# Latent attention's heads in pairs, two heads' outputs at a time, gates before roots, fillers moved

## What is computed

```
s = einsum('bhqd,bhkd->bhqk', qblk, k) * scale;  p = softmax(s);  o = einsum('bhqk,bhkv->bhqv', p, v)

a = where(incl, einsum('bhnid,bhnjd->bhnij', q_dec, k_inv), 0);  o_intra = einsum('bhnij,bhnjv->bhniv', a, v)
def step(s, xs):                                   # per chunk
    o = einsum('bhcd,bhdv->bhcv', qd_c, s)
    s = s * ge_c[..., None] + einsum('bhcd,bhcv->bhdv', ke_c, v_c)

gla = rms_norm(gla, o_norm) * silu(gg)             # even layer
o   = rms_norm(o, o_norm) * silu(g)                # odd layer
rms_norm(x, w) = x * rsqrt(mean(x * x) + EPS) * w
```

## Time and profile before

| | |
|---|---|
| runs | 2077.41, 2098.91, 2096.75 us, median 2096.75 |
| profiled execution | 2104.82 us, span 2103.0 us |
| busy shares | PE 94%, PEld 83%, DVE 55%, ACT 49%, POOL 7% |
| mean granted clock of TensorE | 0.977 of 2.4 GHz |
| DMA | 254.55 MB, mean 121 GB/s |

### The profile page before, as it was taken

The page is one execution under the profiler, slowest core; times in us unless marked ns, Lnnn a source line. Parts: engine busy times, 40 slices in busy tenths (PEclk is TensorE's granted clock), DMA queues, the critical chain, the costliest instruction groups (busy, mean ns, idle before and its releaser), DMA issues.

```text
span 2103.0 us, 40763 instructions
## 1 busy us (share of the span) xinstructions
PE 1983.4 (94%) x16442; PEld 1737.9 (83%) x16442; DVE 1164.9 (55%) x1809; ACT 1030.9 (49%) x1624; POOL 156.6 (7%) x151
## 2 busy tenths in 40 slices
PE   6999999899999999999889999999989998999997
PEld 5884588787788788878778889999879998788997
DVE  4421578654643343355345667667757656667654
ACT  5333367634432233244644456555747655356653
POOL 0000100001000000100044310010020001011000
PEclk9999999889999999999999999999999999899999
DMA  8340268541233333232200056665436664325653
GB/s 270 96 125 30 70 207 249 156 121 50 80 93 97 90 91 99 83 99 82 71 4 4 24 144 187 183 186 145 132 100 188 186 179 138 101 66 145 186 174 110
DMA packets 441801, 254.55 MB, mean 121 GB/s; under 512 B 10817, under 2 KB 440513, under 8 KB 441537
## 3 DMA queue, kind: packets, MB, share of 16 engines
q1 hardware_dynamic: 441664, 252.59, 41.0%
HBM read 251.51 MB, written 1.05 MB: 120 GB/s over the span
## 4 chain that ended last, share of the span: by engine, by line
PE 84%; DVE 9%; ACT 4%; issue 2%; DMA 1%; POOL 0%; DVEq 0%; ACTq 0%; SPq 0%; POOLq 0%
PE bank L380 21%; PE bank L382 20%; PE bank L381 20%; PE bank L372 4%; PE bank L601 2%; PE bank L602 2%; DVE weights_lo L330 2%; ACT weights_hi L323 1%; PE bank L939 1%; PE bank L1170 1%; PE bank L1980 1%; PE bank L609 1%; DVE h L2604 1%; DMA ring<-ada_w 1%; PE bank L2005 1%
## 5 line engine op out<-in xcount | busy, mean ns | idle before, releaser
L330 DVE TENSOR_TENSOR weights_lo<-ring,weights_hi 128x1024 fp32r<-128x1024 f32 x472 | 578.2, 1229 | 353.5 <-ACT weights_hi L323 349.4
L323 ACT ACTIVATE weights_hi<-ring 128x1024 fp32r<-128x1024 f32 x472 | 495.7, 1054 | 383.8 <-PE bank L382 359.4
L380 PE MATMUL bank<-x_hi,weights_hi 128*128 128x256 f32 (+1 forms) x2024 | 639.0, 316 | 31.9 <-DVE x_lo L2560 11.0
L381 PE MATMUL bank<-x_lo,weights_hi 128*128 128x256 f32 (+1 forms) x2024 | 629.0, 311 | 0.0
L382 PE MATMUL bank<-x_hi,weights_lo 128*128 128x256 f32 (+1 forms) x2024 | 628.6, 311 | 0.0
L380 PEld LDWEIGHTS bank<-x_hi,weights_hi 128*128 128x128 f32 x2024 | 381.2, 188 | 67.5 <-issue 27.8
L382 PEld LDWEIGHTS bank<-x_hi,weights_lo 128*128 128x128 f32 x2024 | 381.7, 189 | 23.6
L381 PEld LDWEIGHTS bank<-x_lo,weights_hi 128*128 128x128 f32 x2024 | 381.9, 189 | 23.0 <-issue 1.4
L380 PE MATMUL bank<-hidden_hi,weights_hi 128*128 128x256 f32 (+1 forms) x864 | 270.4, 313 | 5.7 <-DVE hidden_lo L2881 3.2
L382 PE MATMUL bank<-hidden_hi,weights_lo 128*128 128x256 f32 (+1 forms) x864 | 269.9, 312 | 0.0
L381 PE MATMUL bank<-hidden_lo,weights_hi 128*128 128x256 f32 (+1 forms) x864 | 268.5, 311 | 0.0
(11 more groups left out here) (358 smaller groups left out, 2338.3 us busy)
## 6 DMA issues: line engine op xcount, KB each, us to landing
ring<-mlp_w SPq DMA_DIRECT2D x128, 512.0 KB, 3.9
ring<-ada_w SPq DMA_DIRECT2D x96, 512.0 KB, 4.6
ring<-w_ffn_in SPq DMA_DIRECT2D x88, 512.0 KB, 4.0
ring<-w_ffn_out SPq DMA_DIRECT2D x32, 512.0 KB, 3.6
ring<-gdn_w_in SPq DMA_DIRECT2D x24, 512.0 KB, 3.9
ring<-even_w_in SPq DMA_DIRECT2D x18, 512.0 KB, 4.1
ring<-w_out SPq DMA_DIRECT2D x16, 512.0 KB, 3.7
ring<-w_in_a SPq DMA_DIRECT2D x14, 512.0 KB, 3.8
```

What stands on the lines that cost most here:

```text
L323: nc.scalar.activation(w_hi[:, g % AHEAD, :], ring[:, g % RAW, :], ACT.Copy).then_inc(hi_done[g % AHEAD].sem, 1)
L330: nc.vector.tensor_tensor(w_lo[:, g % AHEAD, :], ring[:, g % RAW, :], w_hi[:, g % AHEAD, :].bitcast(F32), ALU.subtract).then_inc(lo_done[g ...
L380: pe.matmul(dst, lhs[0](k), rhs[0](k), start=start and k == 0, stop=False)
L381: pe.matmul(dst, lhs[0](k), rhs[1](k), start=False, stop=False)
```

## The change

- `Attention` for the even layer goes through heads in pairs: for each query block an even and an odd head after one another. The value products of both are issued after the second one, alternating between them, into the two partition halves of one bank, with one signal and one copy of 128 partitions. There are four buffers for transposed probabilities.
- GLA's outputs are made for two heads at once: the score products of both, fillers, the wait for the states, then the state products of both heads alternately, in banks 2 and 3. Heads 2 and 3 wait until both banks are copied.
- In both mixers DVE multiplies outputs by norm weight and gate first, then by the root. In the odd layer logarithms and exponentials alternate.
- Fillers are added, moved ahead of waits or made fewer.

```diff
@@ -615,6 +615,8 @@
                         late()
+                    if t == 2:
+                        keep_busy(pe, 3, 10)
                     if t < self.n // 2:
@@ -911,11 +913,11 @@
-                self.units, self.scale, self.p, self.pt = units, scale, room[0:2], room[2:4]
+                self.units, self.scale, self.p, self.pt = units, scale, room[0:2], room[2:6]
                 n = len(units)
-                self.b = {s.sem: s.take(n) for s in (att_scores, att_max, att_exp, att_probs, att_turned, att_probsT,
-                                                    att_mixed, att_out)}
-                self.masked = room[4:6]
+                self.b = {s.sem: s.take(n) for s in (att_scores, att_max, att_exp, att_probs, att_turned, att_probsT)}
+                self.b |= {s.sem: s.take(n // 2) for s in (att_mixed, att_out)}
+                self.masked = room[6:8]
                 self.before = Linear.last
@@ -939,7 +941,7 @@
                     if j == 0:
-                        keep_busy(pe, 1, 3)
+                        keep_busy(pe, 1, 11)
                     if j >= 0:
@@ -949,13 +951,17 @@
                         side.pe(pe, i)
-                    if j >= 0:
-                        u = self.units[j]
+                    if j >= 0 and j % 2 == 1:
+                        pair = j // 2
                         self.wait(pe, att_probsT, j)
-                        self.wait(pe, att_out, j - 2)
-                        r = u["rows"]
-                        product(pe, bank[j % 2][r, 0:P], lambda b: u["v"][b], lambda b: self.pt[j % 2][:, b * P:(b + 1) * P],
-                                len(u["v"])).then_inc(att_mixed.sem, 1)
+                        self.wait(pe, att_out, pair - 2)
+                        nb = len(self.units[j]["v"])
+                        for b in range(nb):
+                            for x in (j - 1, j):
+                                u = self.units[x]
+                                ins = pe.matmul(bank[pair % 2][u["rows"], 0:P], u["v"][b], self.pt[x % 4][:, b * P:(b + 1) * P],
+                                                start=b == 0, stop=b == nb - 1)
+                        ins.then_inc(att_mixed.sem, 1)
@@ -980,11 +986,10 @@
                         ins.then_inc(att_max.sem, 1)
-                    if i >= 2:
-                        j = i - 2
-                        self.wait(dve, att_mixed, j)
-                        nc.vector.tensor_copy(self.units[j]["out"], bank[j % 2][self.units[j]["rows"], 0:P])\
-                            .then_inc(att_out.sem, 1)
+                    if i >= 2 and i % 2 == 1:
+                        pair = (i - 2) // 2
+                        self.wait(dve, att_mixed, pair)
+                        nc.vector.tensor_copy(self.units[i - 2]["out"], bank[pair % 2][:, 0:P]).then_inc(att_out.sem, 1)
                     if side is not None:
@@ -1005,8 +1010,8 @@
                         self.wait(act, att_turned, j)
-                        self.wait(act, att_mixed, j - 2)
-                        nc.scalar.activation(self.pt[j % 2][:, 0:nk], bank[6 + j % 2][:, 0:nk], ACT.Copy)\
+                        self.wait(act, att_mixed, (j - 4) // 2)
+                        nc.scalar.activation(self.pt[j % 4][:, 0:nk], bank[6 + j % 2][:, 0:nk], ACT.Copy)\
                             .then_inc(att_probsT.sem, 1)
@@ -1024,21 +1029,23 @@
-        room = [a[:, 2 * i, :] for i in range(4)]
+        room = [a[:, i, :] for i in range(6)]
         mla_units = []
         for q0, k0, kn in ((0, 0, T), (LAT, LAT, CTX)):
-            for hd in range(MH):
+            for first in range(0, MH, 2):
                 for q in range(q0, q0 + LAT, P):
-                    r = slice((hd % 2) * MV, (hd % 2 + 1) * MV)
-                    mla_units.append(dict(q=qT[0:MQK, hd, q:q + P], k=kT[0:MQK, hd, k0:k0 + kn],
-                                          v=[vt[:, b, hd * MV:(hd + 1) * MV] for b in range(k0 // P, (k0 + kn) // P)],
-                                          rows=r, out=mix[r, hd // 2, q:q + P]))
+                    for par in range(2):
+                        hd = first + par
+                        mla_units.append(dict(q=qT[0:MQK, hd, q:q + P], k=kT[0:MQK, hd, k0:k0 + kn],
+                                              v=[vt[:, b, hd * MV:(hd + 1) * MV] for b in range(k0 // P, (k0 + kn) // P)],
+                                              rows=slice(par * MV, (par + 1) * MV), out=mix[:, first // 2, q:q + P]))
         mla = Attention(mla_units, MQK ** -0.5, room)
         def pe_mla(pe):
             def ready(pe, i):
-                hd = i * P // LAT
-                if i % (LAT // P) == 0 and hd < MH:
+                hd = 2 * (i // 4) + i % 2
+                if i % 4 < 2 and hd < MH:
                     pe.wait_ge(rope_done.sem, 2 + hd // 2)
...
@@ -1151,25 +1158,27 @@
                 pair(i)
-            keep_busy(pe, 4, 13)
-            for hd in range(GH):
-                f, hh = hd // 2, hd % 2
-                if hd == 0:
+            for f in range(GH // 2):
+                if f > 0:
+                    pe.wait_ge(G["outs"], 2 * f)
+                for hh in range(2):
+                    hd = 2 * f + hh
+                    for tb in range(TB):
+                        pe.matmul(bank[2 + hh][:, tb * P:(tb + 1) * P], gv[:, tb, hd * P:(hd + 1) * P], ascore[:, hd, tb, :],
+                                  start=tb == 0, stop=False, skip_group_check=True)
+                if f == 0:
+                    keep_busy(pe, 4, 9)
                     pe.wait_ge(G["states"], 2 * GFB)
-                    pe.wait_ge(G["masked"], 4 * GFB)
-                if hd >= 2:
-                    pe.wait_ge(G["outs"], hd - 1)
-                b = bank[2 + hd % 2]
-                for tb in range(TB):
-                    t = slice(tb * P, (tb + 1) * P)
-                    pe.matmul(b[:, t], gv[:, tb, hd * P:(hd + 1) * P], ascore[:, hd, tb, :], start=tb == 0, stop=False,
-                              skip_group_check=True)
                 for z in range(2):
                     for n in range(1, NCH):
                         c = ORDER[z][n]
-                        ins = pe.matmul(b[:, chunk(c)], states[z][half(hh), f, n, :], qdec[half(hh), GFB * z + f, chunk(c)],
-                                        start=False, stop=z == 1 and n == NCH - 1, skip_group_check=True)
-                ins.then_inc(G["sums"], 1)
+                        for hh in range(2):
+                            ins = pe.matmul(bank[2 + hh][:, chunk(c)], states[z][half(hh), f, n, :],
+                                            qdec[half(hh), GFB * z + f, chunk(c)], start=False, stop=z == 1 and n == NCH - 1,
+                                            skip_group_check=True)
+                            if z == 1 and n == NCH - 1:
+                                ins.then_inc(G["sums"], 1)
             for hd in range(GH):
@@ -1275,11 +1284,13 @@
             for hd in range(GH):
+                dve.wait_ge(G["outs"], hd + 1)
+                nc.vector.scalar_tensor_tensor(out=mix[:, 4 + hd, :], in0=gout[:, hd, :], scalar=vector("gla_o_norm"),
+                                               in1=gg[:, hd, :], op0=ALU.mult, op1=ALU.mult).then_inc(G["gated"], 1)
+            for hd in range(GH):
+                dve.wait_ge(G["gated"], hd + 1)
                 dve.wait_ge(G["roots"], GH + hd + 1)
-                link(dve, nc.vector.scalar_tensor_tensor(out=mix[:, 4 + hd, :], in0=gout[:, hd, :],
-                                                         scalar=vector("gla_o_norm"), in1=groot[:, hd, :],
-                                                         op0=ALU.mult, op1=ALU.mult))
-                nc.vector.tensor_tensor(mix[:, 4 + hd, :], mix[:, 4 + hd, :], gg[:, hd, :], ALU.mult).then_inc(G["merged"], 1)
+                nc.vector.tensor_tensor(mix[:, 4 + hd, :], mix[:, 4 + hd, :], groot[:, hd, :], ALU.mult).then_inc(G["merged"], 1)
@@ -1524,7 +1535,7 @@
         def pe_rest0(pe):
-            keep_busy(pe, 4, 15)
+            keep_busy(pe, 4, 12)
             pe.wait_ge(G["roots"], GH)
...
@@ -1708,10 +1719,10 @@
                 lin, i = (odd_lin, n) if n < NB_CONV else (sg_lin, n - NB_CONV)
+                if n == 2:
+                    keep_busy(pe, 3, 8)
                 odd_tiles.wait(pe, n)
                 width = odd_width(n)
-                if n == 2:
-                    keep_busy(pe, 3, 7)
                 lin.free(pe, i)
@@ -1938,9 +1949,10 @@
                 pe.wait_ge(gdn_tables.sem, 16)
+                pe.wait_ge(OS["logs"], 2 * QKB)
+                keep_busy(pe, 2, 7)
                 pe.wait_ge(OS["cumsd"], 2)
                 pe.wait_ge(OS["ktok"], QKB)
-                keep_busy(pe, 7, 4)
             for z, u in units(p):
...
@@ -2440,22 +2452,25 @@
                 nc.scalar.activation(as_heads(obuf(osq, i)), two_heads(i), ACT.Square).then_inc(OT["squares"], 1)
-            for i in range(4):
```

(37 more changed lines are left out.)

## The result

| | kernel before | changed kernel |
|---|---|---|
| median (fastest to slowest) | 2098.05 us (2077.41 to 2102.24), 6 runs | 2064.35 us (2058.14 to 2069.15), 6 runs |
| profiled execution | 2104.82 us, span 2103.0 | 2063.23 us, span 2061.4 |
| mean granted clock | 0.977 | 0.987 |

The ratio is 0.9844, with a 95% interval of 0.9813 to 0.9875: 1.6% faster. By the profiled executions the change took 41.6 us out of the span, by the medians 33.7. The table cuts both spans at the same instructions, read from the starts and ends of the instructions in the two traces. The last column is the range over the eleven other profiled executions of this study that have the changed kernel's code in that stage. It says which differences one execution can show. The kernel before has one profiled execution, and it is 6.8 us slower than that kernel's median.

What follows compares the result with a forecast made beforehand. TensorE was taken to bound the kernel, with 84% of the chain that ended last. The terms sum to 44.5 us, taking the profiled 2104.82 to 2060; the median, 8 us lower, was put at 2052, range 2035 to 2071.

Steps and rivals of the forecast that it cites:

- Pairs of heads: Attention: two heads' value products issued alternately; 8.7 us gained with 512 keys, 3.2 with 256, in all 11.9 (8 to 13).
- rival 3: Attention: column pairs do not overlap their weight loads, a pair costs 2.04 us as now, 11.9 us go: 2064; chance 0.04.
- Clock at attention's start: Attention's first probabilities: eight more fillers inside TensorE's 4.18 us wait avoid the cold clock; 2.0 us gained (1 to 2.3).
- Outputs: Linear attention's outputs: alternating row halves, sums end sooner, one part cold after a new wait; 17 us gained (11 to 20).
- Gates: Merges of both mixers: gate product moved ahead of the root, with fewer fillers; 2.4 us and 3.5 us gained.
- Odd projection's filler: Before the odd projection: 7 fillers moved from behind the wait to ahead of it; 2.4 us gained (1 to 2.6).
- Delta rule's filler: Before the delta rule: seven fillers ahead of the wait replace 4 cold ones behind it; 3.0 us gained (1.5 to 3.5).
- Start: Kernel start: 10 fillers fit a 4.82 us wait and cold rows go faster; 1.0 us gained (0 to 1.7).
- Last projection: Before the last projection: 5 fillers in a wait make the cold stretch from 1788.4 cheaper; 1.3 us gained (0 to 1.7).
- Rival 1: Attention: vector engine or ring binds once it gets shorter, giving 4 of the 11.9 us: 2060; chance 0.14.
- Rival 2: Linear attention's output stage stays cold to its end: 11 in place of 17 us, fillers 2 us more: 2060; chance 0.15.
- Rivals 4 and 5: Whole kernel: gains given back to DMA and new waits, about 2080, chance 0.04; attention's clock falls, slower, 2179, chance 0.03.

## Why the prediction was right, and where its steps were off

The mechanisms were right where most of the gain lies, in the pairs of heads and in the outputs. The sum was 44.5 us; the profiled executions give 41.6, the medians 33.7, a quarter less. The time forecast, 2052, is 12 us below the measured 2064.35. By the profiled pair, 2.9 of these are the sum. The rest is the base: I set the gain against the median of the three runs shown, 8 us below the profiled execution, while the changed kernel's median lies 1 us above its own. That the sum came within 3 us of 41.6 is in part luck. The delta rule's filler, the start and the outputs gave 8.4 us less than forecast. The pairs gave 2.0 more, and 1.7 us came from a stretch at half clock inside the odd projection, which no term had.

- **Pairs of heads**: 11.9 forecast, 13.9 measured. The price of a pair was right (0.95 forecast, 1.02 measured). Mis-sized: the scores' 0.2 us behind each value product, and the reserve of 1.0 us taken for the 256-key part, where vector engine and ring did not bind. I had no term for the scores. The Trainium skill (TensorEngine Tiling (Array Packing), Key Properties) says that changing the tiling mode drains the engine, and the 0.2 us behind each 64-column product agree with it, though no run isolates it.
- **The Trainium skill's sentence on column pairs** (rival 3: weight loads overlap only where the row group differs) is not what this chip did. Two heads in the two column halves, all rows in use, took 16 instructions in 1.02 us, where one head alone took 8. Alternating mattered with 512 keys alone (1.51 in turn), and with 256 not at all. Why one head's 8 cost 1.02 us and two heads' 16 in turn 1.51 stays open.
- **Clock at attention's start**: 2.0 forecast. The stage with the long filler and single heads (138.86) against before (141.30) gives 2.4, but the kernel with the old, short filler had a full clock there too (124.49 us). The low clock falls ahead of the stage in one execution and into it in another. That the filler did it is not shown. In five of the other executions, all with a low clock shortly before, the long filler was the last thing to end there, and TensorE did not wait at all.
- **Outputs**: 17 forecast, 14.6 in the profiled pair and 13.6 to 19.5 over the executions. The forecast's form held: first group warm, a wait of 2.1 us (2.2 forecast), one part cold behind it. Which part was mis-sized: cold ran 10.2 us, over score products, state products and half the sums. Without the wait the clock held in both executions with four banks. With the wait filled it held in the only one, as it did in one of eight with the wait open; so the wait is where it fell, and whether it does differs between executions.
- **Gates**: 2.4 and 3.5 forecast, 2.8 and 3.9 measured. Each merge ends at the later of operand and fillers, and the runs show it. The order of the gates alone gives 1.5 at each place (7.67 to 6.12; 11.66 to 10.15, where it is together with the alternated logarithms and exponentials), the shorter fillers alone nothing, both 2.8 and 3.9. My expectation before that run added them up instead, and missed.
- **Odd projection's filler**: 2.4 forecast and 2.4 measured, as its block n = 2 starts 35.45 us earlier, where the projection had started 33.04 earlier. But in the kernel with the old fillers, which ran at full clock, the block came only 0.8 us later. The other 1.6 us are the half clock (from 924.8) that the fillers had in the profiled execution before.
- **Delta rule's filler**: 3.0 forecast, 0.45 lost (7.23 us before, 7.68 after, and 7.68 or 7.69 in the seven other executions where these fillers ran cold). The step that failed is "seven ahead of the wait take 3.2 us and fit it": they are themselves behind a wait for the activation engine's logarithms, which left them no room, so they ended after the data, one of the signs named for being wrong. The 1.05 us that my later expectation gave them came from the clock inside the projection. Started earlier they gave 3.9 us, in two executions.
- **Start**: 1.0 forecast, 1.5 lost in the profiled pair. The spread of this stage over the executions is 4.4 us, so neither is measured.
- **Last projection**: 1.3 forecast. The low clock at 1788 is gone in the changed kernel's trace, but the stage's spread of 11 us hides what it is worth. A half clock there is in both profiled executions without this filler (3.4 us at 1788.4 before, 6.8 us at 1753.1 in the kernel with the old fillers) and in none of the eleven with it.
- **Rival 1** showed its mark only at the end (the ring on the chain for 6.4 us) and cost less than 1 us. **Rival 2** came by half in the profiled execution, and by more in the two with 20.34 us. **Rivals 4 and 5** did not come: attention ran at full clock with 0.59 to 1.02 us of dense value products in each pair.

## What to carry to other kernels

Pair up half-array products wherever two are at hand: issued alternately, two heads cost what one did. Price a filler by what it waits for itself, and by the later of its end and the operand's: shortening it gives nothing until the operand comes sooner, and the other way round. A short wait in the middle of a stream can cost more in clock than in time (2.1 us of wait were followed by 10.2 us or more at half clock in five of eight executions); free banks so that it goes, here for 9 us, rather than halve it. And compare two traces product by product before you give a microsecond to an edit: one stretch at half clock in one of them, 1.7 us here, is as large as most terms of this sum.

## What the runs showed of the hardware

One kernel's executions differ in where the granted clock is 0.50, by whole episodes of 3.4 to 17 us. The changed kernel's whole time varies by 11 us; that the episodes make all of that is not shown. State products with 64 rows, alternating row halves, ran 112 in a stream at 0.058 us each at full clock; 28 on one row half took 0.117 each, and the clock fell at their end (453.7), or within them (443.1, with a head at a time in the changed kernel). And 17 us at half clock from 365.3 in the changed kernel, against 10.2 and 3.4 in that stretch before, left its stage as long as it was (68.22 and 68.18 us): there TensorE's clock did not set the end. Two executions with 27 and 24 us at half clock took 71.5 and 72.3 us, so this cover has a limit, and not by the length alone.
